# Three of each step's 16 dots go to TensorE in 16 turns of 384 columns, and VectorE's ring has 7 slots

## The reference, cut to what matters

```
def block(args):
    xb, ib, wb = args
    u = jnp.take(expert_u, ib, axis=0)
    a = jax.nn.gelu(jnp.einsum('nd,nhkd->nhk', xb, u), approximate=False)
    coef = (a * wb).astype(xb.dtype)
    return jnp.einsum('nhk,nhkd->nd', coef, jnp.take(expert_v, ib, axis=0))
```

## Time and profile before

| what | value |
|---|---|
| median of 3 runs | 4646.01 us (4642.32 to 4651.24) |
| the profiled execution's own time | 4648.74 us |
| its span in the profile | 4646.9 us |
| mean granted TensorE clock | 0.914 of full |
| busy over the span: PE, DVE, POOL, ACT | 82%, 62%, 33%, 15% |
| transfers, mean over the span | 374 GB/s |
| line 2376, the ring's dots | 224 of 2.28 us |
| line 947 and 950, gathers of the stage | 256 of 1 MB |

### The profile page before, as it was taken

One profiled execution on the slowest core, in us unless ns is written; L12 is line 12 of the kernel. 1 busy time (PEld: TensorE's weight loads), 2 busy tenths in 40 slices (PEclk: granted clock), 3 DMA queues, 4 the chain that ended last, 5 costly groups with the idle time before them and its releaser, 6 DMA issues.

```text
span 4646.9 us, 34164 instructions
## 1 busy us (share of the span) xinstructions
PE 3831.5 (82%) x11856; PEld 1841.0 (40%) x11856; DVE 2874.0 (62%) x3871; ACT 716.0 (15%) x1674; POOL 1525.3 (33%) x1102
## 2 busy tenths in 40 slices
PE   4978989999788899899999896233455799999896
PEld 0333334444344444444444343223344544444342
DVE  2312017988433401267777887999999866666567
ACT  0111001100132210110111011111386400000000
POOL 0000003443333200134542456656665322222223
PEclk7989999999899999999999998666676899999998
DMA  9998998998999878899999999999999799999998
GB/s 375 377 349 302 358 356 335 358 360 355 375 408 409 358 262 319 328 369 385 363 361 393 388 390 389 409 382 409 402 401 397 275 409 396 421 421 422 421 422 341
DMA packets 385255, 1736.82 MB, mean 374 GB/s; under 512 B 26432, under 2 KB 30048, under 8 KB 231248
## 3 DMA queue, kind: packets, MB, share of 16 engines
q0 software_dynamic: 150336, 1079.53, 57.5%
q1 hardware_dynamic: 234768, 655.39, 37.1%
HBM read 1703.00 MB, written 33.13 MB: 374 GB/s over the span
## 4 chain that ended last, share of the span: by engine, by line
PE 35%; DMA 30%; DVE 23%; issue 9%; ACT 1%; POOL 1%; SPq 0%; DVEq 0%; another core or an unknown queue 0%; POOLq 0%; PEldq 0%; ACTq 0%
PE ps L983 27%; DVE big L2376 8%; DMA zone<-in_peer_u,sel 5%; DMA big<-in_peer_u,sel 4%; DMA zone<-in_peer_v,sel 4%; DMA big<-in_w_in 3%; DMA big<-in_peer_v,sel 3%; DMA big<-in_peer_v,zone 2%; DMA big<-in_w_ada 2%; PE ps L1083 2%; DVE activations L2417 1%; PE ps L1142 1%; DMA activations<-in_peer_u,sel 1%; DVE work L1936 1%; DMA activations<-in_peer_v,sel 1%
## 5 line engine op out<-in xcount | busy, mean ns | idle before, releaser
L983 PE MATMUL ps<-big,activations 128*128 128x512 f32 x4032 | 1767.5, 598 | 61.0 <-DMA big<-in_w_in 13.0
L983 PEld LDWEIGHTS ps<-big,activations 128*128 128x128 f32 x4032 | 764.6, 191 | 1046.4 <-issue 981.3
L950 POOL DMA_INDIRECT big<-in_peer_u,sel x224 | 360.8, 1611 | 247.3 <-DVE zt L2376 106.5
L2082 DVE CUSTOM_DVE_ANT_0 big<-big 128x2048 f32<-128x2048 f32 x128 | 289.2, 2290 | 40.3 <-DMA big<-in_peer_u,sel 38.6
L2021 DVE SCALAR_TENSOR_TENSOR big<-big,work 128x2048 f32<-128x2048 f32 x115 | 270.5, 2352 | 65.2 <-DMA big<-in_peer_v,sel 62.3
L918 POOL DMA_INDIRECT big<-in_peer_u,sel x128 | 215.8, 1686 | 284.8 <-DVE zone L2082 247.6
L2011 DVE CUSTOM_DVE_ANT_0 big<-big 128x2048 f32<-128x2048 f32 x114 | 259.8, 2289 | 72.5 <-DMA big<-in_peer_u,sel 71.3
L2376 DVE CUSTOM_DVE_ANT_0 big<-big,zone 128x2048 f32<-128x2048 f32 x112 | 251.6, 2283 | 3.1 <-DMA big<-in_peer_u,sel 2.7
L2376 DVE CUSTOM_DVE_ANT_0 big<-big,activations 128x2048 f32<-128x2048 f32 x112 | 251.6, 2283 | 0.3
L2417 DVE SCALAR_TENSOR_TENSOR activations<-big,work,activations 128x2048 f32<-128x2048 f32 x75 | 176.3, 2351 | 111.8 <-DMA big<-in_peer_v,sel 111.4
L879 POOL DMA_INDIRECT big<-in_peer_v,sel x96 | 169.1, 1761 | 195.7 <-DVE big L2021 147.0
(11 more groups left out here) (289 smaller groups left out, 4807.9 us busy)
## 6 DMA issues: line engine op xcount, KB each, us to landing
big<-in_w_in SPq DMA_DIRECT2D x84, 2048.0 KB, 10.7
big<-in_w_ada SPq DMA_DIRECT2D x48, 2048.0 KB, 12.7
big<-in_w_out SPq DMA_DIRECT2D x24, 2048.0 KB, 11.6
big<-in_peer_w_query SPq DMA_DIRECT2D x24, 2048.0 KB, 10.0
misc<-in_peer_v SPq DMA_DIRECT2D x43, 1024.0 KB
zt<-in_peer_v SPq DMA_DIRECT2D x43, 1024.0 KB
zone<-in_peer_v SPq DMA_DIRECT2D x42, 1024.0 KB
big<-in_w_branch_a SPq DMA_DIRECT2D x12, 2048.0 KB, 19.2
```

The lines of the kernel that those rows point to most:

```text
L950: pool.indirect_dma_start(u_slot(m), None, eu, bass.IndirectOffsetOnAxis(ap=sel[:, t % 2, k:k + 1], axis=0)).then_inc(u_in[m % UR], 16)
L983: ins = nc.tensor.matmul(bank(bk), acts[:, k, b * P:(b + 1) * P], w[:, n % WS, k], start=(start and k == 0), stop=(stop and k == KT // 2 - 1))
L2082: V.tensor_tensor_reduce(out=slot(m), in0=slot(m), in1=hcur, scale=1.0, scalar=0.0, op0=ALU.mult, op1=ALU.add, accum_out=dots_0[:, m:m + 1 ...
```

## The change

Three tiles of a step instead of two are turned rows (`TURNED` = 3), so VectorE has 13 ring dots and not 14 in a step. The three tiles need three places, and the third is taken from the ring, which has 7 slots (`UR`). A turn takes one piece of 128 columns of each of the three tiles, 384 columns, so that there are 16 turns of a step and not 8 (`TURNS`). The products of a turn are one matmul of 384 columns and not two of 256. The items stand behind turns 2, 5, 8, 11 and 14 of 16, and not 1, 2, 4, 5 and 7 of 8; the exponentials stand behind turn 3 and not 1.

```diff
-UR = 8
-TURNED = 2
+UR = 7
+TURNED = 3
 STEP_DOTS = TOPK - TURNED
-TURNS = KT // 2
+TURNS = KT
...
-        turned_rows_at = (bg(8 * D, D), bg(9 * D, D))
+        turned_rows_at = (bg(7 * D, D), bg(8 * D, D), bg(9 * D, D))
...
-            return at[:, x % 4 * CH:(x % 4 + 1) * CH]
+            return at[:, x % 4 * CH:x % 4 * CH + TURNED * P]
...
             if PH < t < STEPS_U:
-                behind = (1, 2, 4, 5, 7)
+                behind = (2, 5, 8, 11, 14)
...
                 pe.wait_ge(t_free, T_DOTS + x + 1)
-                for i in range(2):
-                    for k in range(TURNED):
-                        ins = nc.tensor.transpose(bank(4 + x % 4)[:, (TURNED * i + k) * P:(TURNED * i + k + 1) * P],
-                                                  turned_rows_at[k][:, (2 * j + i) * P:(2 * j + i + 1) * P], ident[:, :])
+                for k in range(TURNED):
+                    ins = nc.tensor.transpose(bank(4 + x % 4)[:, k * P:(k + 1) * P], turned_rows_at[k][:, j * P:(j + 1) * P], ident[:, :])
                 ins.then_inc(t_done, 1)
...
-                for i in range(2):
-                    ins = nc.tensor.matmul(products_bank(t), h_tile(t // PH, 2 * j + i), turned_tile(x)[:, i * TURNED * P:(i + 1) * TURNED * P],
-                                           start=(j == 0 and i == 0), stop=(j == TURNS - 1 and i == 1))
-                ins.then_inc(turn_mul, 1)
+                nc.tensor.matmul(products_bank(t), h_tile(t // PH, j), turned_tile(x), start=(j == 0), stop=(j == TURNS - 1)).then_inc(turn_mul, 1)
...
-                nc.scalar.activation(turned_tile(x), bank(4 + x % 4), ACT.Copy).then_inc(t_free, 1)
+                nc.scalar.activation(turned_tile(x), bank(4 + x % 4, TURNED * P), ACT.Copy).then_inc(t_free, 1)
...
-                    if j == 1:
+                    if j == 3:
                         top_exps(2 * PH + t + 1)
```

## The result

The changed kernel takes 4720.80 us (median of 6 runs, 4715.56 to 4735.24); the kernel before, on the same chip, 4641.09 (6 runs). The ratio is 1.0179 (95% interval 1.0163 to 1.0194): 79.7 us slower. The forecast was 4735, with a range of 4702 to 4765. The profiled execution of the changed kernel took 4734.72 us for a sum of 4737.4: 86.0 more than the 4648.74 of before, where the sum said 88.7. By the medians the change is +79.7, so the sum is 9.0 too large. That it looks closer in the profiled executions is partly luck: that of the changed kernel lies 13.9 us above the median of six runs, that of the kernel before 7.7.

The account below looks back on a forecast made before the run. VectorE was taken to set the pace, with 2.3 us slack in the loop through GpSimd. 7.4 - 1.9 + 9.5 + 71.7 + 2.0 = +88.7 on 4648.74 gave 4737.4, so 4735 for the median; range 4702 to 4765.

Parts of the forecast that it names:

- VectorE alone: Step time if only VectorE counted: one plain dot less (-2.2 us), longer diagonals (+0.3), 40.0 us after 41.95.
- An ordinary step: Steps 2 to 8: the loop through GpSimd takes 43.3 us against 41.95 before, +1.35 in each of 7, +9.5.
- E: The end of a step's exponentials, when ScalarE resumes its copies; predicted 15.8 us after the step's first dot.
- A building step: Steps 9 to 14: three items delay the last transposes; period 53.9 us, 11.95 more in each of six, +71.7.
- The first steps: Steps 0 and 1: step 0 +7.4 us from later exponentials and a longer loop; step 1 -1.9, loop hidden.
- The last step: Stage's end: the last block's first gather waits for the last transposes and is used at 27.4 after E, +2.0 us.
- The landing, against the page: Ring's first tile, issue to landing: 9.1 us from the rows; the page's 4.4 would make the sum about +29.
- the rival: A tile lands fast once nothing else is on its way, 4.7 us less: +29, 4675 us; 5 in 100.
- The clock: Rival: TensorE's copies and products run at the lower clock throughout, +53 on top, 4788 us; 6 in 100.
- the other side: Rival: VectorE stays the limit in every step, faster, -31 us, 4615; 4 in 100.
- about 310: Sign in building steps: the granted transfer rate falls to about 310 GB/s, 16.9 MB in 54 us.
- its bounds on the low side: The sum with all terms at their low bounds, given as +57 us, 4703.

Follow-up runs that it names:

- the edits above: Changed kernel with three ring tiles gathered first, later diagonals and one item between: 4622.3 us; with step 0's exponentials also ahead of ScalarE's copies: 4619.45 us.

## Why the prediction was right, by its own steps

**VectorE alone, 40.0 us.** Not seen in the changed kernel, where it is hidden, but with the ring ahead of the turned rows. The diagonals over 384 columns are 0.55 us, as taken.

**An ordinary step.** The mechanism held; 43.3 was too short by 0.8. E at 16.1 (15.8 predicted); last transposes from there 12.3 (11.5), since three turns ran at the lower clock and not two: products start 1.92 us apart at 3126.49 and 3128.41 and are 0.81 long only from 3130.19 on; GpSimd's first turned row at E + 13.1 (12.1); three rows 6.4 (6.0); landing 8.55 (9.4). The terms make 44.2 for this step; over seven steps it was 44.03. The prediction's "+1.35 for each" was +2.04.

**A building step.** 53.9 was predicted and 52.9 found in the step shown, 52.44 in the mean. E + 22.3 for the last transposes (21.7), GpSimd at E + 23.1 (22.2): nearly as derived, from items 5.41 us apart. Two terms were mis-sized and partly cancel. The three turned rows took 3.75 us and not 6.8, since VectorE had run dry and an issue was 0.94 to 0.96 long. Then the tile landed in 10.3 and not 9.1. The second seems to follow from the first: from the first turned row's issue (3471.73) to the fourth tile's landing are 14.05 us, of which four tiles of 1.05 MB at 421 GB/s are 10.0, an estimate from the rate measured with the ring first. By it, tiles that are issued faster mostly queue behind each other; no run varied the issue alone. That the issue depends on VectorE's idleness, which the loop itself makes, was missing from the prediction, and is the largest part of the -9.4 in this row of the table.

**The first steps.** The size was right (+6.8 for +7.4), the split was not. The exponentials end 29.65 us behind the first dot for 23.85 before, +5.8 where 4.0 was derived; from there to the next first dot only +1.0 came where 3.4 was derived, since the first turned row was issued at E + 10.4 and not E + 12, and that tile landed in 8.5 us and not 9.1. Step 1 gave the -1.9, hidden behind another block's norm.

**The last step.** The gather for the last block was issued at E + 18.4 (18.3 predicted) and used 7.5 us later (9.1): +0.5 for +2.0.

**The landing, against the page.** The Trainium skill's figure of 4.4 us for such a tile ("DMA: Bandwidth & Descriptors", section "Anatomy of one DMA — SWDGE (gpsimd) path") would have given +29, and +86.0 was measured. The landings of 8.55 and 10.3 us are of tiles with hardly more than the three turned rows ahead of them. The prediction said that a landing under 8 us would be wrong, and the last step has one of 7.5, of a tile issued when GpSimd had been idle for 7.5 us:

```profile
3677.01 2.98 POOL L970 DMA_INDIRECT big<-in_peer_u,sel  x1 [7.50 <-PE ps L1377]
...
3684.52 2.29 DVE L2389 CUSTOM_DVE_ANT_0 big<-big,activations 128x2048 f32<-128x2048 f32 x1 [2.08 <-DMA big<-in_peer_u,sel]
```

The issue itself is 2.98 us of these 7.5. From its end the lone tile needs 4.5 us, where the one of before at 3216.04, issued in 1.91, needed 7.2, and the one in the building step above, behind three others, 9.4. So the rival is right that a lone tile is fast, and the page's 4.4 is near the 4.5 if one counts from the end of the issue; counted from its start, as the prediction's sum does, it is 7.5 here. The rival fails because no tile on the loop is alone: the turned rows are always ahead.

**The other rivals.** The clock fell no lower than forecast, but for a turn longer in the ordinary step shown: 0.50 for three turns and then 1.00. VectorE as the limit throughout, the other side, came about only with the edits above, and then gave 18 to 21 us less than the kernel before, for that rival's 31. Of the forecast's signs one was off in size: the rate in building steps is 335 GB/s for "about 310". The window begins in the end of an ordinary step; over the six building periods alone (3328.17 to 3642.82) it is 324, and the shorter steps account for most of what is left (16.9 MB in 52.4 us are 322). One sum of the prediction is off: its bounds on the low side add up to +55 (4701), not +57, which the result does not touch.

## What to carry to other kernels

When work moves from a busy engine to an idle one, trace the loop that it rides on through every in-order queue (here choice, exponentials, copies, transposes, gathers, ring), and compare its length with the period; a slack of 2.3 us in 41.9 was the warning, though all shares of busy time looked roomy. The number of foreign items in front of the instruction that releases the next queue is a dial: 43.6, 47.1 and 52.4 us a step for none, one and three. Before giving up such a change, reorder the waiting queue: three tiles that depend on nothing late, gathered ahead of the wait, took back 80 us, and placing the items, with the diagonals later, gave 19 more (the two together; later diagonals alone gave nothing).

## What the runs showed of the hardware

GpSimd's issue of a gather varies with what VectorE does. It is 1.91 us at 3143.37, while VectorE does one dot after another, and 0.94 at 3475.48, while VectorE stands idle, for the same line and the same 1 MB. Over the stage of the changed kernel, 69 issues fall wholly into idle time of VectorE, and each lasts 0.93 or 0.94; 53 lie under dots for 95% or more of their length and last 2.20 in the mean (0.94 to 3.02). Mean over line 950, from the costliest groups of the changed kernel's page:

```profile
L950 POOL DMA_INDIRECT big<-in_peer_u,sel x208 | 271.5, 1305 | 314.3 <-DVE qts L2371 141.1
```

and of the kernel with late diagonals and one item, where VectorE hardly waits:

```profile
L950 POOL DMA_INDIRECT big<-in_peer_u,sel x208 | 351.7, 1691 | 197.3 <-DVE zt L2373 80.0
```

The Trainium skill, "SBUF — State Buffer", section "Who interferes with whom", has VectorE and GpSimd share a pair of ports under an exclusive lock, for which a VectorE instruction with two inputs in SBUF competes when GpSimd reads SBUF. The dot has two such inputs, and the rows agree in direction. The same section also says, with the reason marked as inferred, that `tensor_tensor` did not seem to stall a DMA in a probe; issues of 2.20 us in the mean under the two-input dot point the other way. Whether the lock is the cause was not tested apart.
